# Two chained two-layer transformer blocks on one core: the input loaded in column quarters, fewer zero products, and the last down products finished row tile by row tile

## The reference, cut to what matters

```python
for l in range(2):                       # first block
    h = rms_norm(x, norm_mix[l])
    z = h @ w_in[l]                      # 1024 x 4768
    ...
    x = x + y @ w_out[l]
    h = rms_norm(x, norm_ffn[l])
    x = x + (silu(h @ w_gate[l]) * (h @ w_up[l])) @ w_down[l]
for layer in range(2):                   # second block, other mixer
    h = h + hybrid_mixer(rmsnorm(h, norm_mix[layer]), ...)
    h = h + swiglu(rmsnorm(h, norm_ffn[layer]), w_gate[layer], w_up[layer], w_down[layer])
return rmsnorm(h, final_norm)            # row-wise, over the 1024 columns
```

## Time and profile before

| | us |
|---|---|
| median of three runs | 1432.07 |
| the profiled execution: its time | 1432.51 |
| the profiled execution: its span, first to last instruction | 1430.7 |
| TensorE busy | 1421.5 |
| VectorE busy | 927.7 |
| ScalarE busy | 804.5 |
| GpSimd busy | 80.5 |

### The profile page before, as it was taken

How to read it: one execution, slowest core, us unless ns; L and a number is a source line. 1 busy time by engine, 2 the same in 40 slices (tenths; PEclk the granted TensorE clock), 3 DMA queues, 4 the chain that set the end, 5 groups by cost and what they waited for, 6 DMA issues and landing times.

```text
span 1430.7 us, 20211 instructions
## 1 busy us (share of the span) xinstructions
PE 1421.5 (99%) x7938; PEld 1201.8 (84%) x7938; DVE 927.7 (65%) x1288; ACT 804.5 (56%) x1311; POOL 80.5 (6%) x86
## 2 busy tenths in 40 slices
PE   9999999999999999999999999999999999999998
PEld 8887888888888878888889988888888988888886
DVE  5698765565467988555556788655555788655553
ACT  6775555444467654544445788544445688544443
POOL 0122200000002220000000000000000000000001
PEclk9999999999999999999999999999999999999999
DMA  8653456666365445576564435566554544566661
GB/s 284 213 161 119 156 164 204 197 191 191 108 224 177 148 137 167 158 221 194 186 187 144 128 119 162 177 209 206 190 183 120 156 148 142 180 193 192 191 188 49
DMA packets 178702, 245.47 MB, mean 172 GB/s; under 512 B 18976, under 2 KB 130224, under 8 KB 178608
## 3 DMA queue, kind: packets, MB, share of 16 engines
q1 hardware_dynamic: 178416, 244.11, 54.7%
q10 hardware_dynamic: 192, 0.08, 0.0%
HBM read 243.10 MB, written 1.05 MB: 171 GB/s over the span
## 4 chain that ended last, share of the span: by engine, by line
PE 99%; DVE 0%; ACT 0%; issue 0%; DVEq 0%; ACTq 0%
PE acc L566 19%; PE acc L569 19%; PE acc L572 19%; PE misc L566 10%; PE misc L569 10%; PE misc L572 10%; PE misc L667 3%; PE misc L933 1%; PE misc L734 1%; PE misc L709 1%; PE misc L675 1%; PE misc L886 0%; PE misc L887 0%; PE misc L884 0%; PE misc L688 0%; PE misc L577 0%
## 5 line engine op out<-in xcount | busy, mean ns | idle before, releaser
L1434 DVE TENSOR_TENSOR w_lo<-w_raw,w_hi 128x1024 fp32r<-128x1024 f32 (+3 forms) x472 | 555.0, 1192 | 267.9 <-ACT w_hi L1024 266.3
L1024 ACT ACTIVATE w_hi<-w_raw 128x1024 fp32r<-128x1024 f32 (+3 forms) x472 | 478.9, 1031 | 271.6 <-PE misc L572 164.4
L566 PE MATMUL acc<-w_hi,h_hi 128*128 128x512 f32 (+3 forms) x832 | 208.8, 373 | 1.0 <-ACT w_hi L1024 1.0
L569 PE MATMUL acc<-w_lo,h_hi 128*128 128x512 f32 (+3 forms) x832 | 201.1, 364 | 0.2 <-DVE w_lo L1434 0.2
L572 PE MATMUL acc<-w_hi,h_lo 128*128 128x512 f32 (+3 forms) x832 | 200.9, 364 | 0.0
L566 PE MATMUL misc<-w_hi,h_hi 128*128 128x512 f32 x640 | 175.5, 396 | 0.0
L569 PE MATMUL misc<-w_lo,h_hi 128*128 128x512 f32 x640 | 171.5, 390 | 0.0
L572 PE MATMUL misc<-w_hi,h_lo 128*128 128x512 f32 x640 | 171.5, 390 | 0.0
L569 PEld LDWEIGHTS acc<-w_lo,h_hi 128*128 128x128 f32 x832 | 147.9, 188 | 22.9 <-DVE w_lo L1434 0.7
L572 PEld LDWEIGHTS acc<-w_hi,h_lo 128*128 128x128 f32 x832 | 148.0, 188 | 21.8
L566 PEld LDWEIGHTS acc<-w_hi,h_hi 128*128 128x128 f32 x832 | 142.2, 188 | 22.5 <-ACT w_hi L1024 2.5
(11 more groups left out here) (229 smaller groups left out, 1182.5 us busy)
## 6 DMA issues: line engine op xcount, KB each, us to landing
w_raw<-in_w_in SPq DMA_DIRECT2D x92, 512.0 KB, 4.3
w_raw<-in_w_gate SPq DMA_DIRECT2D x176, 256.0 KB, 2.9
w_raw<-in_w_up SPq DMA_DIRECT2D x176, 256.0 KB, 3.1
w_raw<-in_w_down SPq DMA_DIRECT2D x88, 512.0 KB, 3.4
w_raw<-in_w_out SPq DMA_DIRECT2D x40, 512.0 KB, 3.8
w_raw<-in_w_in SPq DMA_DIRECT2D x32, 388.0 KB, 3.5
w_raw<-in_w_in SPq DMA_DIRECT2D x16, 336.0 KB, 4.5
w_raw<-in_w_proj_a SPq DMA_DIRECT2D x8, 512.0 KB, 4.2
```

The source lines that it names most:

```text
L566: pe.matmul(dst, st[0][:, k, t * P:(t + 1) * P], rhs, start=first, stop=False)
L569: pe.matmul(dst, st[0][:, k, t * P:(t + 1) * P], rhs, start=False, stop=False)
L1024: act.activation(w_hi[:, g % RING, 0:w], w_raw[:, g % RING, 0:w], ACT.Copy)\
L1434: dve.tensor_tensor(w_lo[:, g % RING, 0:w], w_raw[:, g % RING, 0:w], w_hi[:, g % RING, 0:w].bitcast(F32), ALU.subtract)\
```

## The change

x is loaded in four column quarters, each behind one weight slot. The zero products go from 16 to 11. ScalarE's queue loads the identity ahead of the first gains. In the first layer TensorE does `nT`*i*+1 only when slot *i* of `mla0` is finished: nT0, slot 0, nT1, slot 1, nT2, slot 2, nT3, slot 3. In the last layer the last down products go row tile by row tile, and the adds, squares, sums and powers of the final norm follow that order. The diff, cut to its core:

```diff
@@ beginning @@
-            for _ in range(16):
+            for _ in range(11):
                 pe.matmul(misc[2][:, 0:P], warm, warm, start=True, stop=True)
...
-            def x_half(half):
-                cols = slice(half * 512, half * 512 + 512)
+            def x_quarter(i):
+                cols = slice(i * 256, i * 256 + 256)
...
-                    if g == 0:
-                        x_half(1)
+                    if g < 3:
+                        x_quarter(g + 1)
...
-                        pe.wait_ge(x_in[i // 2], 16)
+                        pe.wait_ge(x_in[i], 16)
...
                     if item[0] == "slot":
                         run_slot(layer, item[1], item[2])
+                        if layer == LAYERS[0] and item[1] == "mla0" and item[2] < 3:
+                            shared(layer, f"nT{item[2] + 1}")
                     elif item[1] in ("nT2", "nT3") and layer[0] == 1:
+                        continue
+                    elif item[1] in ("nT1", "nT2", "nT3") and layer == LAYERS[0]:
                         continue
...
+            act.dma_start(ident, A["const"][:, C_ID:C_ID + P]).then_inc(ident_in, 16)
             act.dma_start(first[0:8, :], A["norm_mix"][0:1, :].rearrange("a (k p) -> (a k) p", p=P)).then_inc(mix_in, 16)
-            act.dma_start(ident, A["const"][:, C_ID:C_ID + P]).then_inc(ident_in, 16)
@@ end, TensorE @@
+                def last_rows(g):
+                    for t in range(NT):
+                        down_sweep(g, 10, down_cells(g, 10, (0,), (t,)), t == 0)
+                        down_sweep(g + 1, 10, down_cells(g + 1, 10, (0,), (t,))).then_inc(*PE.mark(f"x_half{t}"))
+                        mm = down_sweep(g, 10, down_cells(g, 10, (1,), (t,)))
+                        if t:
+                            mm.then_inc(*PE.slot("used", g))
+                        mm = down_sweep(g + 1, 10, down_cells(g + 1, 10, (1,), (t,)))
+                        mm.then_inc(*(PE.slot("used", g + 1) if t else PE.mark("x_row0")))
...
-                last_down(g + 6)
+                if layer == LAYERS[-1]:
+                    last_rows(g + 6)
+                else:
+                    last_down(g + 6)
@@ end, ScalarE @@
+            final_square(0, 0)
+            final_square(0, 1)
+            final_square(1, 0)
+            final_row(0)
+            final_square(1, 1)
+            final_row(1)
@@ end, VectorE @@
+                if layer == LAYERS[-1]:
+                    dve.wait_ge(*PE.at(layer, "x_half0"))
+                    residual(layer, [(0, 0, acc[0])], ["x_ffn0"])
+                    dve.wait_ge(*PE.at(layer, "x_row0"))
+                    residual(layer, [(1, 0, acc[2])], ["x_ffn2"])
+                    dve.wait_ge(*PE.at(layer, "x_half1"))
+                    residual(layer, [(0, 1, acc[1])], ["x_ffn1"])
+                    row_sum(0)
+                    dve.wait_ge(*PE.of("used", BASE[layer] + o.slots - 1))
+                    residual(layer, [(1, 1, acc[3])], ["x_ffn3"])
+                    return
...
             for t in range(NT):
+                if t:
+                    row_sum(1)
                 dve.wait_ge(fin_r, t + 1)
@@ end, GpSimd @@
             for t in range(NT):
                 pool.wait_ge(*DV_.at(LAYERS[-1], f"x_ffn{t}"))
                 pool.tensor_tensor(hrow[:, t, 0:512], x[:, t, 0:512], gains[:, 0:512], ALU.mult).then_inc(fin_gain, 1)
-            for t in range(NT):
                 r = small[:, RS + t:RS + t + 1]
                 pool.wait_ge(fin_sum, t + 1)
                 pool.tensor_tensor(r, r, small[:, 192:193], ALU.pow).then_inc(fin_r, 1)
```

More of the change, by code:

```diff
@@ L414, in build @@
         by = {"act": AC, "dve": DV_}
-        x_in = [sem(f"x_half{half}_loaded") for half in range(2)]
+        x_in = [sem(f"x_quarter{i}_loaded") for i in range(4)]
         c_in, lb_in, pos_in = sem("const_loaded"), sem("lb_loaded"), sem("positions_loaded")
@@ L462, in _ @@
         def _(sp):
-            def x_half(half):
-                cols = slice(half * 512, half * 512 + 512)
-                sp.dma_start(x[:, :, cols], A["x"][:, cols].rearrange("(t p) d -> p t d", p=P)).then_inc(x_in[half], 16)
+            def x_quarter(i):
+                cols = slice(i * 256, i * 256 + 256)
+                sp.dma_start(x[:, :, cols], A["x"][:, cols].rearrange("(t p) d -> p t d", p=P)).then_inc(x_in[i], 16)
             def row(name, l, n):
@@ L548, in layer_loads @@
                         params(LAYERS[LAYERS.index(layer) + 1])
-            x_half(0)
+            x_quarter(0)
             for layer in LAYERS:
@@ L1153, in body_a @@
                     split_until(layer, 4)
-                    act.wait_ge(x_in[0], 16)
-                    act.wait_ge(x_in[1], 16)
+                    for i in range(4):
+                        act.wait_ge(x_in[i], 16)
                 squares(layer, "nT")
@@ L1409, in _, with final_square, final_row @@
                     body((block, l))
-            for half in range(2):
-                for t in range(NT):
[L1412 to L1417, removed]
+            def final_square(t, half):
+                v = slice(half * 512, half * 512 + 512)
+                c = 2 * t + half
+                act.wait_ge(*DV_.at(LAYERS[-1], f"x_ffn{2 * half + t}"))
+                act.activation(xdump[:, t, v], x[:, t, v], ACT.Square, scale=D ** -0.5,
+                               accum_out=small[:, c:c + 1]).then_inc(fin_ms, 1)
+            def final_row(t):
                 act.wait_ge(fin_r, t + 1)
@@ L1540, in _, with row_sum @@
             n = [3]
+            def row_sum(t):
+                dve.wait_ge(fin_ms, 2 * t + 2)
+                r = small[:, RS + t:RS + t + 1]
+                dve.scalar_tensor_tensor(out=r, in0=small[:, 2 * t:2 * t + 1], scalar=EPS_B,
+                                         in1=small[:, 2 * t + 1:2 * t + 2], op0=ALU.add, op1=ALU.add)\
+                    .then_inc(fin_sum, 1)
             def link(ins):
```

## The result

The changed kernel takes 1443.75 us in the median of six runs (1440.6 to 1444.55), against 1432.12 before (1431.99 to 1432.88): 11.6 us slower, a ratio of 1.0076 with a 95% interval of 1.0066 to 1.0087. Before, the runs lie within one microsecond of each other; after, they spread over four. The profiled execution took 1444.55 us, at the slow end of these; its mean granted clock is 0.992, and over the six runs the clock lies between 0.992 and 0.997, where the run at 0.997 is the fastest. (The clock also reads 0.50 in the last microseconds of a span, as in the earlier trace rows, with TensorE out of work. So a mean of 0.998 or 0.999 is that of a kernel whose clock stays up until the tail.)

The account below looks back on a forecast made before the run. TensorE, busy 1421.5 of 1430.7 us, bounds the kernel, so a late start moves the end. Head +7.18 (8.44 - 1.26) and tail -0.6 give +6.58, hence 1438.6 us; range 1436.5 to 1444.5, the forecast's own case 1437.8 to 1440.4.

Parts of the forecast that it names:

- the case that I took as the likeliest: Whole kernel: chain in slots 1 to 3 at the full clock, 1438.6 us, 0.46% slower; chance 0.70.
- Start: First microseconds: fewer zero products and swapped loads start the gains' turn at 6.0, not 7.26, gaining 1.26 us (0.66 to 1.56).
- T: Start of the gains' turn (L580) on TensorE, forecast at 6.0 us, bounds 5.7 and 6.6, against 7.26 before.
- Slots 0 to 3 and slot 4: First layer: each slot's chain waits for its turn, 5.28 then 4.55 us; slot 4's `cross` at T + 20.59, 8.44 us later.
- The rival's price: Lower clock in slots 0 to 3: up to 1.66 us per slot, 6.6 for four, 1445.2 us; chance 0.15.
- The warm-up: Zero products at the start: fewer of them risk leaving TensorE at the throttled clock; only slot 0 slow gives 1440.3 us.
- The turns hide: Slots 1 to 3: added idle time under 0.62 us per slot; fully hidden the kernel ends at 1430.2; chance 0.08.
- the gains come late: Start: the gains' DMA behind the identity lands about 7.2, so the start gains nothing, 1439.9 us; chance 0.07.
- End: Final norm and stores: first store issued earlier, second lands alone without contention, -0.6 us, bounds nothing and -0.7.

Follow-up runs that it names:

- the start alone: The kernel before with only 11 zero products and the identity's load ahead of the first gains: 1431.45 us, ratio 0.9994.
- the tail alone: The kernel before with only the last down products row tile by row tile, squares, sums and powers in that order: 1431.66 us, ratio 0.9995.

## Why the prediction was right in its direction, and which step failed

The direction, the place and the range held; the time did not come from the case that I took as the likeliest. I forecast 1438.6, with 1437.8 to 1440.4 for that case, and it is 1443.75.

- **Start.** Right in its number, 6.04 against 6.0, and that by luck. I took the gains' load for what T waits for. In every trace here T is 0.07 us ahead of the end of the last zero product's record, 6.11 in the changed kernel; I had put that end at 5.7, the start of a 23rd load, and left the last product's own time out. Where the products quickened sooner, T came sooner, 5.73, 5.47 and 5.06 with the same 11 products and the same loads, so both loads were there by 5.06. With this start T thus varies by 1 us from profile to profile, and single profiles don't price it. In the runs the start alone is 0.9 us by the medians, against 1.26. How much of it needs the swapped loads, no run separates; before, the identity landed at 6.6.
- **Slots 0 to 3 and slot 4.** Right as a chain, and shown by the kernel with five zero products ahead of `high`, which holds the clock up: 5.28 and 4.55 us, `cross` of slot 4 at T + 20.52, 1439.05 us in all. That weights split behind h make it long is shown by the kernel that splits them ahead (3.53).
- **The failed step** is the one under it: that the products of these slots run at the full clock. In the profiled execution they ran at half of it from slot 0's `low` to the end of slot 3, and one of the prediction's own signs of being wrong, products of 336 columns at double their time, was there (1.12 us for four instead of 0.61). I gave the fall a chance of 0.15, with the 1.04 us gap before slot 0 as the evidence against it. But that row was of a kernel in which four more transposes filled the front of that gap and nothing idled after slot 0; in the changed kernel the stretch before slot 0 is 1.65 us by the profile's idle column, and 1.4 to 1.6 come again in every slot, with a further wait ahead of `cross` in slots 0 and 1. That the idle time takes the clock down, and not the missing zero products, is shown: 16 of them do not hold it, products put into the idle time do, and 11 are enough where only the 1.04 us gap before slot 0 is left. The rival's price, 1.66 per slot and 6.6 for four, was a little high: measured 5.3 in the profiled execution (slot 4 at T + 25.90 instead of T + 20.59), 4.7 between the medians, since the clock is not down all the time in every run, and in this one not in slot 0's `high`.
- **The warm-up.** The Trainium skill, "TensorE: Matmul & The Clock Gate", Part 1, says that the throttled clock is the default and activity releases it. The trace agrees, with loads of 333 ns at the start and 192 ns later. The risk that I had put at the shorter warm-up was the smaller part: of the 5.3 us, 0.5 were lost there, since the first transposes still ran at the lower level and h_hi of slot 0 came at T + 1.42, against T + 0.91 in the kernel that holds the clock up. The other 4.8 came with the idle time behind it.
- **The turns hide, the gains come late.** Neither: every `high` of slots 1 to 3 waited, and T was as forecast.
- **End.** -0.6 forecast, -0.4 between span and last product in the trace, -0.7 by the medians of the tail alone, within its noise. The working had two errors that nearly cancel. I gave the later store the 2.7 us of the earlier trace rows; asked for alone, that store shows

```profile
DMA to landing us min/median/max: 3.3/3.3/3.3
```

  and the 2.7 belong to the first. And a lone store takes 2.6, not the 2.1 that I worked out. The contention that is saved is 0.7 us, and the second store is issued 0.2 later than forecast behind the last product, since VectorE's half of row tile 0 took 1.20 us and held up the second sum. The Trainium skill's figures ("DMA: Bandwidth & Descriptors", "Anatomy of one DMA — SWDGE (gpsimd) path") give an estimate of 3.2 us for the lone store; the rows have 2.6, so here the estimate is 0.6 too long. Its fit is for DMAs issued by GpSimd, and these stores are issued by SyncE: I should not have leaned on it.
- **Not settled:** what makes the clock fall in slot 0 in one profile and in slot 1 in another, and whether the length of the warm-up has a part in it. No run here separates that.

## What to carry to other kernels

Before a step of TensorE is put behind another one, write down which engines work in between and in which order *their* programs have it: here a turn that moved behind a slot pulled two engines' splits into a chain of 4.6 us around 2.3 us of work, although nothing was moved on those engines. When TensorE is made to idle at short intervals, price its work at both levels of the clock. If the idle time can't be removed, zero products in it can be cheaper than none; better still is to have everything that does not hang on the late operand done ahead of it.

## What the runs showed that I had not expected

- The clock fell in slots with idle stretches of 1.65 us and less (in the changed kernel TensorE was busy for 2.23 of the 4.00 us from 6 to 10, and it fell at about 10.6). With one stretch of 0.85 to 1.28 us in each slot (weights split ahead) it stayed up in all eleven runs.
- With the same slots the fall comes in different places: the changed kernel lost the clock from slot 0 on in its profile, the one with 16 zero products from slot 1. And the same program spreads: six runs of the changed kernel had mean clocks from 0.992 to 0.997.
- VectorE's scaling of a 128x512 tile took 1.20 us beside GpSimd's product over the same shape, and 0.75 in the same kernel with GpSimd idle. VectorE's add of x and a bank took 0.69 in the same neighbourhood and before.
